# Expert rows by 0/1 matrices from SBUF for all 32 experts, and an earlier use of the modulation weights

## What is computed

```python
mod = jax.nn.silu(c) @ w_ada[l] + b_ada[l]                     # 6 x 1024 values
shift1, scale1, gate1, shift2, scale2, gate2 = jnp.split(mod, N_MOD, axis=-1)
...
h2 = modulate(rmsnorm(x, norm2_w[l]), shift2, scale2)
...
p_group, g_idx = lax.top_k(group_probs, 1)                     # one of 4 groups
p_exp, e_local = lax.top_k(jax.nn.softmax(e_logits, axis=-1), TOP_K)   # 2 of its 8 experts
flat_e = (g_idx * EXPERTS_PER_GROUP + e_local).reshape(-1)     # 32 experts
xs = xf[tok]                                                   # rows sorted by expert
hid = jax.nn.silu(lax.ragged_dot(xs, w1, group_sizes)) * lax.ragged_dot(xs, w3, group_sizes)
ys = lax.ragged_dot(hid.astype(xs.dtype), w2, group_sizes) * gate...
return jax.ops.segment_sum(ys, tok, num_segments=n)
```

## Time and profile before

| | us |
|---|---|
| median of 3 runs | 980.49 (980.26 to 982.2) |
| the profiled execution | 980.23, its span 978.4 |
| PE busy | 904.7 (92%) |
| DVE busy | 450.9 (46%) |
| ACT busy | 263.9 (27%) |
| POOL busy | 147.9 (15%) |
| moved by DMA | 295.00 MB, mean 302 GB/s |
| chain that ended last | PE 60%, DMA 28%, DVE 4%, issue 3%, POOL 3%, ACT 2% |

### The profile page before, as it was taken

How to read it: one execution, slowest core, us unless ns; L and a number is a source line. 1 busy time by engine, 2 the same in 40 slices (tenths; PEclk the granted TensorE clock), 3 DMA queues, 4 the chain that set the end, 5 groups by cost and what they waited for, 6 DMA issues and landing times.

```text
span 978.4 us, 12487 instructions
## 1 busy us (share of the span) xinstructions
PE 904.7 (92%) x5081; PEld 573.7 (59%) x5081; DVE 450.9 (46%) x734; ACT 263.9 (27%) x372; POOL 147.9 (15%) x147
## 2 busy tenths in 40 slices
PE   7999999979899999898875999898989899999998
PEld 4688887747753444333322343332433699999887
DVE  2357625246544443232321333332323778888843
ACT  1226423225311110101110011101111646556532
POOL 0005864012120000000000000000000102222300
PEclk9999999989999999999996999999999999999999
DMA  9988229395999999999999999999999665554411
GB/s 341 277 177 206 86 91 340 102 330 190 423 372 407 405 405 415 396 408 405 402 421 414 402 403 403 411 415 402 420 421 364 196 191 193 194 196 175 172 44 44
DMA packets 87785, 295.00 MB, mean 302 GB/s; under 512 B 11198, under 2 KB 35254, under 8 KB 63015
## 3 DMA queue, kind: packets, MB, share of 16 engines
q1 hardware_dynamic: 82167, 286.10, 78.0%
q10 hardware_dynamic: 3152, 5.96, 1.6%
q0 software_dynamic: 2400, 2.04, 0.8%
HBM read 297.81 MB, written 2.10 MB: 307 GB/s over the span
## 4 chain that ended last, share of the span: by engine, by line
PE 60%; DMA 28%; DVE 4%; issue 3%; POOL 3%; ACT 2%; DVEq 0%; ACTq 0%; POOLq 0%
DMA ring<-in_w_dram 25%; PE ps L940 10%; PE ps L1059 6%; PE ps L1060 6%; PE ps L1061 6%; PE ps L493 6%; PE ps L963 5%; PE ps L943 4%; PE ps L577 4%; PE ps L472 3%; PE ps L477 2%; PE ps L508 2%; DMA ring<-in_w_in_dram 2%; PE ps L982 1%; DMA ring<-in_w_ada_dram 1%
## 5 line engine op out<-in xcount | busy, mean ns | idle before, releaser
L943 PE MATMUL ps<-ring,proj 128*64 128x512 f32 x288 | 129.6, 596 | 15.0 <-DMA ring<-in_w_dram 15.0
L940 PE MATMUL ps<-ring,proj 128*64 128x512 f32 x272 | 126.4, 606 | 1.8 <-issue 1.6
L1576 DVE TENSOR_TENSOR proj<-RQ,ps 64x512 f32<-64x512 f32 x32 | 22.1, 690 | 209.5 <-PE ps L925 115.6
L943 PE MATMUL ps<-arena,proj 128*64 128x512 f32 x224 | 104.0, 614 | 9.2 <-DMA arena<-in_w_dram 9.2
L940 PE MATMUL ps<-arena,proj 128*64 128x512 f32 x240 | 110.1, 602 | 2.3 <-issue 2.3
L1738 DVE TENSOR_TENSOR w_l<-ring,w_h 128x2048 fp32r<-128x2048 f32 x33 | 75.5, 2292 | 44.8 <-ACT w_h L2053 44.8
L1059 PE MATMUL ps<-h_h,w_h 128*128 128x256 f32 x336 | 95.1, 283 | 0.0
L1061 PE MATMUL ps<-h_h,w_l 128*128 128x256 f32 x336 | 95.1, 283 | 0.0
L1060 PE MATMUL ps<-h_l,w_h 128*128 128x256 f32 x336 | 95.1, 283 | 0.0
L2018 ACT CAST MX_r<-RQ 64x512 fp32r<-64x512 f32 x64 | 39.5, 618 | 195.5 <-DVE RQ L1593 194.7
L2258 POOL DMA_INDIRECT proj<-rows_scratch,idx x30 | 28.2, 941 | 377.6 <-PE ps L925 356.2
(11 more groups left out here) (327 smaller groups left out, 1655.4 us busy)
## 6 DMA issues: line engine op xcount, KB each, us to landing
ring<-in_w_dram SPq DMA_DIRECT2D x108, 1024.0 KB, 26.7
arena<-in_w_dram SPq DMA_DIRECT2D x84, 1024.0 KB, 27.0
ring<-in_w_ada_dram SPq DMA_DIRECT2D x11, 2048.0 KB, 10.5
ring<-in_ffn_w_in_dram SPq DMA_DIRECT2D x22, 1024.0 KB, 7.6
ring<-in_w_in_dram SPq DMA_DIRECT2D x6, 2048.0 KB, 14.6
ring<-in_ffn_w_out_dram SPq DMA_DIRECT2D x5, 2048.0 KB, 7.7
arena<-in_w_in_dram SPq DMA_DIRECT2D x2, 2048.0 KB, 21.9
ring<-in_w_out_dram SPq DMA_DIRECT2D x2, 2048.0 KB, 8.8
```

Source lines behind the costliest of these rows:

```text
L940: pe.matmul(ps[0:SLOTS, :], XTe[i % 2][:, k, :], u1[:, k, :], start=(k == 0), stop=(k == 7))
L943: t = pe.matmul(ps[64:64 + SLOTS, :], XTe[i % 2][:, k, :], u3[:, k, :], start=(k == 0), stop=(k == 7))
```

## The change

Four things change together.

1. **Rows of all experts by matrix.** The store to `xs`, the table `idx`, the 30 indirect transfers, the two memsets before them, `turn_x` on PE and on DVE and `direct_rows` are gone. In their place PE does `picks(p)` once for two experts: 16 matmuls of 128 x 128 x 128 from the normed rows in SBUF (now `XR`, in the room where the gathered rows were) and `pick`. It stands behind `turn_h(i)` for each even i, and before `places` for the first pair. DVE makes `pick` with one instruction for each expert (`vector_pick`, from `place_of`, which is computed once), and ACT writes the rows of both experts, scaled and shifted, into `XT2` with 8 ACTIVATEs (`scalar_rows`), behind the silu of expert i+1. `up(i)` waits for the bank of `picks` to be emptied by ACT.
2. **Modulation units.** `ada(7)` and `ada(10)` move forward, into level 5 and behind the scores; `column_totals(3)` and `ada(8)` move ahead of `u0`; `ada(9)` moves ahead of `vn`. SP's queue has ada 8 and ada 9 ahead of proj 4.
3. **Slots.** The rotation of the expert units begins with slot 1 (`ring`), so w1 of expert 0 can be loaded once proj 4 is used.
4. w1 and w3 of expert 0 are queued one whole unit after the other.

```diff
@@ slots
-                        (("ada", 6), 0), (("proj", 3), 1), (("ada", 7), 2), (("ada", 10), 0), (("proj", 4), 1), (("ada", 8), 2),
-                        (("ada", 9), 0), (("ada", 11), 2), (("wo", 0), 0), (("wo", 1), 2)):
+                        (("ada", 6), 0), (("proj", 3), 1), (("ada", 7), 2), (("ada", 10), 0), (("ada", 8), 2), (("ada", 9), 0),
+                        (("proj", 4), 1), (("ada", 11), 2), (("wo", 0), 0), (("wo", 1), 2)):
...
-            units.place(name, (4, 5, 6, 1, 0, 2, 3)[i % 7])
+            units.place(name, (1, 4, 5, 6, 0, 2, 3)[i % 7])
@@ PE, first part
                 if level == 1:
                     queries(1)
+                elif level == 5:
+                    ada(7)
...
                     for h in range(4):
                         scores(h)
+                    ada(10)
                 else:
                     project(7)
-                    ada(7)
-                    ada(10)
+                    column_totals(3)
+                    ada(8)
...
             four(("u0",), lambda h: XT[:, 0, h, :], lambda h: VBT[:, 0, h, :])
-            column_totals(3)
             retained(0)
...
             retained(1)
-            ada(8)
+            ada(9)
...
             four(("oq",), lambda h: qkv[:, h, 128:256], lambda h: ST[:, h, :], keep=True)
-            ada(9)
             project(8)
@@ PE, experts
-            def turn_x(i):
-                ps = take("turn_x", i)
-                src = XG[i % 4].rearrange("s (c p) -> s c p", c=8)
...
+            def picks(p):
+
+                if E is main and p == 0:
+                    pe.wait_ge(h2_rows, 2)
+                pe.wait_ge(E.picked, 2 * p + 2)
                 for g in range(2):
-                    ps = take("direct", g)
+                    ps = take("pick", p, g)
                     for c in range(4 * g, 4 * g + 4):
                         o = 128 * (c % 4)
                         for n in range(2):
-                            t = pe.matmul(ps[:, o:o + 128], MX[:, n, c * 128:(c + 1) * 128],
+                            t = pe.matmul(ps[:, o:o + 128], XR[:, n, c * 128:(c + 1) * 128],
                                           pick[:, n, :, :].rearrange("p e s -> p (e s)"), start=(n == 0), stop=(n == 1))
-                    t.then_inc(*mm.up("direct", g))
+                    t.then_inc(*E.mm.up("pick", p, g))
...
                     if k % 4 == 0:
+                        pe.wait_ge(*E.drained("pick", i // 2, k // 4))
                         pe.wait_ge(*(half1 if k == 0 else full1))
...
                 turn_h(i)
-                if i + 2 < high:
-                    turn_x(i + 2)
+                if i % 2 == 0 and i + 2 < high:
+                    picks(i // 2 + 1)
@@ DVE
+            ve.scalar_tensor_tensor(place_of, rank, -SPARE, SM, ALU.add, ALU.mult).then_inc(*vd.up("place_of"))
...
+        def vector_pick(ve, E, i):
+
+            expert, blk = E.jobs[i]
+            if i > 1:
+                ve.wait_ge(*E.mm.of("pick", i // 2 - 1, 1))
+            ve.scalar_tensor_tensor(pick[:, :, i % 2, :], place_of[:, :, expert:expert + 1].to_broadcast([128, 2, SLOTS]),
+                                    SPARE - SLOTS * blk, mid(cst("places")[:, 0:SLOTS]), ALU.add,
+                                    ALU.is_equal).then_inc(E.picked, 1)
...
-                ve.tensor_tensor(XTe[i % 2], ps[:, :].rearrange("p (c s) -> p c s", c=8),
-                                 modc[:, 3, :].unsqueeze(2).to_broadcast([128, 8, SLOTS]), ALU.mult).then_inc(*free("turn_x", i))
-                ve.wait_ge(*E.drained("turn_x", i))
-                ve.tensor_tensor(XTe[i % 2], XTe[i % 2], modc[:, 2, :].unsqueeze(2).to_broadcast([128, 8, SLOTS]),
-                                 ALU.add).then_inc(E.xt_ready, 1)
@@ ACT
-                ac.dma_start(xs[tok(n), :], MX[:, n, :]).then_inc(rows_stored, 16)
...
+        def scalar_rows(ac, E, p):
+
+            for c in range(8):
+                if c % 4 == 0:
+                    ac.wait_ge(*E.mm.of("pick", p, c // 4))
+                b = E.banks.at["pick", p, c // 4][0]
+                i = ac.activation(XT2[:, :, c, :], PS[b][:, 128 * (c % 4):128 * (c % 4) + 128].rearrange("p (e s) -> p e s", e=2),
+                                  ACT.Identity, scale=modc[:, 3, c:c + 1], bias=modc[:, 2, c:c + 1])
+                if c % 4 == 3:
+                    i.then_inc(E.bank_free[b], 1)
...
                 if i + 1 < end and not before_last:
                     up(i + 1)
+                if i % 2 == 0 and i + 2 < end:
+                    scalar_rows(ac, E, i // 2 + 1)
                 high(i)
@@ POOL
-                po.indirect_dma_start(XG[i % 4], None, xs, bass.IndirectOffsetOnAxis(ap=idx[0:SLOTS, col:col + 1], axis=0),
-                                      bounds_check=255, oob_is_err=False).then_inc(E.gathered[i % 4], 16)
@@ SP
             load_ada(10)
-            load_in("proj", 4, 3584)
             load_ada(8)
             load_ada(9)
+            load_in("proj", 4, 3584)
...
-            load_halves(("w1", 0), ("w3", 0))
+            load_halves(("w1", 0))
+            load_halves(("w3", 0))
```

More of the change, by code:

```diff
@@ L21 @@
 MIDDLE = NE // 2
-DIRECT = 2
 SMALL_LOADS = 12 * 16
@@ L986, in combine @@
                     t.then_inc(*E.mm.up("combine", i))
+            picks(low // 2)
             if before_first:
-                direct_rows()
                 before_first()
-            else:
-                turn_x(low)
             up(low)
-            if not before_first:
-                turn_x(low + 1)
             for i in range(low, high):
@@ L1432, in vector_program, with places @@
             ve.tensor_reduce(slot[:, 1, :], pps[1], AX, ALU.add).then_inc(*vd.up())
-            def places(between):
+            def places():
                 ve.wait_ge(*vd.now())
@@ L1616, in vector_experts @@
                     low_part(i - 1)
-                if i + 2 < end:
-                    turn_x(i + 2)
                 if behind_first and i == first:
@@ L2018, in high @@
                     ac.copy(YB[i % 2][own, j, :], YG[own, :]).then_inc(E.high_rows, 1)
+            if E is not main or first:
+                scalar_rows(ac, E, first // 2)
             up(first)
```

129 lines of the change are left out of this document (28 added, 101 removed).

## The result

The changed kernel takes 969.50 us (median of 4 runs, 969.03 to 971.32), the kernel before, beside it, 980.98 (980.26 to 982.2). The ratio is 0.9885, 95% interval 0.9868 to 0.9902. It is 11.5 us faster, where 20 were forecast: 969.5 lies just above the range's upper end of 969.0. The profiled execution took 969.73 us, its span 967.9.

What follows compares the result with a forecast made beforehand. The prediction took the DMA stream of expert weights as the bound, with PE following; the stream would gain 7.0 + 20.6 = 27.6 us, PE only 19.7, so 980.2 - 19.7 = 960.5 us, range 951.5 to 969.

Steps and rivals of the forecast that it cites:

- The first part, 7.0 us: Modulation units, up to up(0): without the wait for ada 8 and the half clock behind it, 7.0 us gained.
- eaten by proj 4: Rival, modulation units: proj 4 lands 3 us later than assumed, only 4 us gained there, time 963.5; chance 0.12.
- Router: The stage of pick and picks before up(0): the change there is worth zero, between -0.5 and +1 us.
- Gathers, 20.6 us: Expert weight stream: without the 30 indirect transfers it runs at 421 GB/s instead of 404, 20.6 us less.
- The rival of cheap gathers: Gathers cost little more than their bytes (5 us), the DMA side stays the bound; 965 to 968, chance 0.18.
- The bound passes to PE: Experts: PE alone 19.7 us earlier, the stream 27.6, so PE is later and 8 us are not seen.
- PE's sum: PE's time to combine(30) if weights were always there: 696.3, less 17.7 for turn_x, plus 53.6 for picks: 732.2 us.
- the middle: Term of PE's time in the experts: from combine(13) to combine(16), with the branch and slow clock, 59.8 us.
- my four reference rounds: Expert rounds from 321.59 to 372.43 us in the kernel before, from which PE's 12.71 us a round was taken.
- The rival of a slower kernel: PE waits for ACT at the start of each even up, 15 times; 45 us added, 1006; chance 0.05.
- the 4 us that I called a bound of the first part: Lower bound of the modulation units' gain, if proj 4 lands as late as the slowest.
- my own sign: The prediction counts as wrong as a whole if combine(30) is not between 724 and 741 us.

Runs made afterwards that it cites:

- e3: The changed kernel with ada(7) moved back on PE and ACT, behind the scores and in front of ada(10); 968.15 us, ratio 0.9849 to the kernel before.
- e7: The changed kernel with picks over the first 128 tokens only, 8 matmuls a pair instead of 16, output wrong; 957.40 us, ratio 0.9748 to the kernel before.
- e1: The kernel before with the 30 indirect transfers left out and nothing else, output wrong; 961.94 us, ratio 0.978 to the kernel before.

## Why the prediction was wrong, point by point

- **The first part, 7.0 us: the step that failed.** It measured 2.2 (1.1 in the profile, where the first 20 us took back the rest). The step reads "ada 7 and ada 10 ... go ahead of `project(7)`, partly into a gap, so I let `project(7)` end 2.9 us later, at 188.8". It ended at 193.8: 6.8 later than before when the shift of 1.1 is taken off, and 3.9 later than I let it. I costed the work of `ada(7)` and never asked when its weights land. The rows for that were in the trace of before, two of SP and the cast of proj 3 on ACT:

```profile
145.43 0.59 SPq L2306 DMA_DIRECT2D ring<-in_w_in_dram  x1
151.33 11.22 SPq L2306 DMA_DIRECT2D ring<-in_w_ada_dram  x2
...
160.51 1.90 ACT L1836 CAST ring_r<-ring 128x2048 fp32r<-128x2048 f32 x1 [3.96 <-DMA ring<-in_w_in_dram]
```

  Proj 3, issued at 145.43, landed only at 160.51, and ada 7 was issued 5.9 us behind it, 2 MB each; the gap that I meant to fill was at 164.1. In the changed kernel ada 7 lands 14.8 us after its issue:

```profile
152.44 27.00 SPq L2241 DMA_DIRECT2D ring<-in_w_ada_dram  x4
```

  The wait is 2.02 us, half clock adds 0.7 in `ada(7)` and 0.9 behind it: 3.6 of the 3.9. e3 moved it, and the projection came 2.6 us earlier. I had allowed for no half clock at a new place; e7 shows that with the wait but without half clock 5.3 us are gained up to the projection. Of the 5.0 us that are missing there 3.9 arise before the end of `project(7)` and 1.1 behind it.
- Proj 4 was let land 10.5 us after `project(7)`; it took 11.5 (SP at 193.89, ACT's cast at 205.34). The DVE chain behind it made `u1` wait 1.26, forecast 1.4. That mechanism was right. The 1.0 us by which the transfer took longer is the 1.1 missing behind `project(7)`; the rival "eaten by proj 4" names this smaller part of the loss, and the larger is that `project(7)` was late.
- **Router**: zero, within the bounds; from the output projection to `up(0)` 49.8 us against 50.0, both with the same clock.
- **Gathers, 20.6 us: right.** e1 measured 20.8; the 64 rows of 4 KB that each gather names, 7.86 MB in all, would have given 18.7. The rival of cheap gathers (967, chance 0.18) is refuted, although 969.5 lies next to its time: with it `up` would still wait for weights at a rate of 404, and neither is seen.
- **The bound passes to PE: right**, shown by e7.
- **PE's sum**, by stages, forecast and measured: `up(0)` to `combine(1)` 50.0 and 51.2; to `combine(13)` 163.9 and 166.4; the middle to `combine(16)` 64.6 and 60.6; to `combine(28)` 166.8 and 169.6; to `combine(30)` 16.9 and 18.0. With the 5.9 us of the late start that is the 9.5 us by which `combine(30)` is late. The rounds are 0.45 us a pair too short in my sum, and the term that was mis-sized is `turn_x` at 0.59 us, 30 times. I took it from one round in which it ran alone. In half of the rounds it ran between the transposes of `turn_h` and cost 0.03 us; on average its removal took 0.27 us from the step, not 0.59, and the wait of `down` (0.22 in each pair) was there before as now. That is 0.64 us a pair too much. The other way, my four reference rounds held a step that comes only once (two transposes at 339.0, about 0.46 us), which made the rounds 0.11 us too long: 0.22 a pair. The picks were sized well, 3.60 to the next step against 3.57.
- The middle was sized 4.0 too long. I took 59.8 from a stretch that itself held waits which the changed kernel has not, as the kernel before shows:

```profile
535.60 1.09 PE L940 MATMUL ps<-arena,proj 128*64 128x512 f32 x1 [2.31 <-issue]
...
545.99 0.61 PE L963 MATMUL ps<-ring,proj 128*64 128x512 f32 x1 [1.31 <-issue]
```

- `scalar_rows` was covered: 458 ns an ACTIVATE although it writes in two pieces, and no wait of `up` for ACT. The rival of a slower kernel is refuted.
- The range was 0.5 us too narrow above. Its upper end rested on the rival of cheap gathers, and the 4 us that I called a bound of the first part was none. By my own sign, `combine(30)` between 724 and 741, the prediction is wrong as a whole, by 0.7 us. Two errors in opposite directions, the rounds (5.4 us in 12 pairs) and the middle (4.0 us), hide each other in part: that PE's sum is off by only 3.6 us is luck.

## What to carry to other kernels

When work is moved forward, ask first when its data lands at the new place, from the row of the load queued ahead of it; a unit put before its data pays the wait and, in three of four traces here, a slow clock behind it. When work is removed, look at it in every kind of round: here it ran beside other work in half of them and cost nothing there. When an order is changed, count the changes of work. And a stretch that is to stand for pure work has to be searched first for waits and for steps that come only once.

## What the runs showed of the hardware

- The same instructions ran at 2.4 or at 1.2 GHz from one execution to the next in the stage with waits and narrow matmuls: 35.4 to 39.7 us in four traces of one code, 35.1 to 38.0 in four of another. Gains of 2 us ahead of it don't show in medians of four to six runs.
- 64 rows of 4 KB to 64 partitions cost the stream of weights 1.5 us from POOL's queue, 2.8 from the weights' own queue, 0.62 by bytes. A gather of which a quarter of the rows arrive cost it 0.69.
- Eight transposes of 64 rows on partitions 64 to 127 ran between four on partitions 0 to 63 and added 0.03 us; with both on partitions 0 to 63 they added 0.50.
- One more change from one kind of matmul to another in a round cost PE 0.15 us, with no wait shown.
